# One decoder layer: the dense products handed out in double portions at every second place of three stages

## Time and profile before

| what | value |
|---|---|
| median of three runs | 1400.93 us (1395.85 to 1408.07) |
| the profiled execution | 1402.41 us |
| its span, first to last instruction | 1400.5 us |
| mean granted TensorE clock, as a share of full speed | 0.957 |
| PE matmuls | 1294.8 us busy, 92% of the span |
| DVE, ACT, POOL | 635.9, 350.2 and 578.0 us busy |
| chain that ended last, share of PE | 84% |
| transfers from HBM | 129.31 MB, 92 GB/s on average |

### The profile page before, as it was taken

One profiled execution on the slowest core, in us unless ns is written; L12 is line 12 of the kernel. 1 busy time (PEld: TensorE's weight loads), 2 busy tenths in 40 slices (PEclk: granted clock), 3 DMA queues, 4 the chain that ended last, 5 costly groups with the idle time before them and its releaser, 6 DMA issues.

```text
span 1400.5 us, 23708 instructions
## 1 busy us (share of the span) xinstructions
PE 1294.8 (92%) x10276; PEld 1205.1 (86%) x10276; DVE 635.9 (45%) x1026; ACT 350.2 (25%) x518; POOL 578.0 (41%) x433
## 2 busy tenths in 40 slices
PE   4989999997858899999997999897999999999999
PEld 4989999886758787877787988886999999999999
DVE  6245655525364444455554532314738710177400
ACT  4231222200451233332322121211332211222210
POOL 1443653311163167656512334221536544455542
PEclk9999999997998898999998999988999999999999
DMA  4311121040322143332341325213222323223232
GB/s 181 105 61 61 60 62 56 36 98 31 105 61 93 38 153 127 137 120 76 106 161 50 113 69 196 61 46 122 91 91 91 91 91 91 91 91 93 95 97 95
DMA packets 42909, 129.31 MB, mean 92 GB/s; under 512 B 3958, under 2 KB 15006, under 8 KB 40621
## 3 DMA queue, kind: packets, MB, share of 16 engines
q1 hardware_dynamic: 38197, 102.62, 23.0%
q0 software_dynamic: 4608, 25.17, 5.0%
HBM read 121.64 MB, written 6.36 MB: 91 GB/s over the span
## 4 chain that ended last, share of the span: by engine, by line
PE 84%; DVE 8%; DMA 4%; ACT 2%; issue 1%; SPq 1%; DVEq 0%; ACTq 0%
PE PS L622 19%; PE PS L624 18%; PE PS L623 18%; PE PS L651 9%; PE PS L914 3%; PE PS L937 2%; DMA M<-w_tiles 2%; PE PS L727 2%; PE PS L923 2%; PE PS L1082 1%; PE PS L1070 1%; DMA M<-state_hgrn 1%; PE PS L763 1%; PE PS L765 1%; PE PS L882 1%
## 5 line engine op out<-in xcount | busy, mean ns | idle before, releaser
L2132 POOL TENSOR_TENSOR WL<-M,WH 128x512 fp32r<-128x512 f32 x314 | 426.4, 1382 | 720.2 <-ACT WH L1183 719.8
L622 PE MATMUL PS<-hH,WH 128*128 128x260 f32 x1360 | 406.6, 299 | 23.5 <-DVE M L1470 13.5
L624 PE MATMUL PS<-hH,WL 128*128 128x260 f32 x1360 | 393.0, 289 | 1.5 <-issue 1.5
L623 PE MATMUL PS<-hL,WH 128*128 128x260 f32 x1360 | 393.0, 289 | 0.0
L622 PEld LDWEIGHTS PS<-hH,WH 128*128 128x128 f32 x1360 | 266.5, 196 | 29.8 <-issue 26.2
L624 PEld LDWEIGHTS PS<-hH,WL 128*128 128x128 f32 x1360 | 265.7, 195 | 1.2 <-issue 1.2
L1183 ACT CAST WH<-M 128x1024 fp32r<-128x1024 f32 x159 | 165.9, 1046 | 402.7 <-DMA M<-w_tiles 267.7
L623 PEld LDWEIGHTS PS<-hL,WH 128*128 128x128 f32 x1360 | 266.0, 196 | 0.5
L624 PE MATMUL PS<-uH,WL 128*128 128x260 f32 x512 | 144.7, 283 | 0.0
L622 PE MATMUL PS<-uH,WH 128*128 128x260 f32 x512 | 144.6, 282 | 0.0
L623 PE MATMUL PS<-uL,WH 128*128 128x260 f32 x512 | 144.1, 281 | 0.0
(11 more groups left out here) (368 smaller groups left out, 2088.9 us busy)
## 6 DMA issues: line engine op xcount, KB each, us to landing
M<-w_tiles SPq DMA_DIRECT2D x159, 512.0 KB, 3.6
M<-x_T SPq DMA_DIRECT2D x8, 520.0 KB, 5.5
M<-cache_win_kv SPq DMA_DIRECT2D x2, 2048.0 KB, 11.2
y_T<-M SPq DMA_DIRECT2D x8, 260.0 KB
con<-tables SPq DMA_DIRECT2D x1, 1475.5 KB, 12.1
M<-state_gla SPq DMA_DIRECT2D x2, 512.0 KB, 8.7
M<-state_hgrn SPq DMA_DIRECT2D x2, 512.0 KB, 11.7
gla_sample<-M SPq DMA_DIRECT2D x2, 512.0 KB, 6.8
```

The source lines that it names most:

```text
L622: mm(out, hi[:, cols], x_hi, start=first, stop=False)
L623: mm(out, hi[:, cols], x_lo, start=False, stop=False)
L624: return mm(out, lo[:, cols], x_hi, start=False, stop=last_k)
L2132: last = p.tensor_tensor(WL8[s][:, c], WR[s][:, c], WH8[s][:, c], ALU.subtract)
```

## The change

In the sections lev, att and s6 a tick with an even number within its section hands out twice the quota (16, 8 and 14 triples), and a tick with an odd number none. The other sections keep their quotas. lev and s6 give the same total as before, att gives 272 triples in place of 268; the units and their order are the same. On DVE the calls of ticks 25 and 39 of s6 stand ahead of softmax_of_round in place of behind it.

```diff
-    for _ in range(_n):
-        CUM.append((CUM[-1] if CUM else 0) + _quota)
+    for _i in range(_n):
+        _now = _quota if _name not in ("lev", "att", "s6") else 2 * _quota * (1 - _i % 2)
+        CUM.append((CUM[-1] if CUM else 0) + _now)
...
+            tick("s6", 25)
             softmax_of_round(0, 1)
-            tick("s6", 25)
             tick("s6", 26)
...
+            tick("s6", 39)
             softmax_of_round(1, 0)
-            tick("s6", 39)
             tick("s6", 40)
```

## The result

| what | before | after |
|---|---|---|
| median of the runs | 1401.98 us (4 runs) | 1430.59 us (4 runs) |
| ratio | 1 | 1.0204 [1.0151, 1.0257] |
| the profiled execution, its span | 1400.5 us | 1431.1 us |
| mean granted clock | 0.957 | 0.946 |

The forecast was 1422 with a range of 1392 to 1447: slower, as forecast, and inside the range. But by stage it was right in one place of three. PE by stretch, first before, then after; the stretches are: decay stage (first score group to the first transposes behind it), the unchanged sections up to the attention, attention, samples, the rest. Columns: stretch, its length, PE busy (instructions), PEclk, DMA share, GB/s.

The account below looks back on a forecast made before the run. PE bounds the kernel, so time moves only with its idle, switches and clock. Decay +30.4, attention -18.9 and samples +9.8 give +21.3 on 1402.4, 1423.7; less 1.5 for the median, 1422, range 1392 to 1447.

Parts of the forecast that it names:

- The bank in the decay stage: Second portion of each level: PE waits 1.1 for DVE's eviction behind the products; with POOL's overlap, 23.8 us in all.
- the rate of 0.39: Decay stage: DVE's products run at 0.39 beside POOL's lower parts, making a level's stall 3.05 or 4.7 us.
- The landing of tiles: Decay stage: tiles land 3.6 after release; with a 1.03 cast POOL begins at about 10.3, meeting the products at 10.4.
- The clock in the decay stage: Decay stage: six stalls of 3 us or more each start a clock fall costing 1.6, 9.6 us in all.
- The joins: Joining two portions saves a pair of switches, 0.19 each: decay -3.0, attention -6.3, samples -3.4 us.
- The attention's waits: Attention: PE's waits for blocks of outputs fall from 9.4 to 4.0, about 2 at the first block, 1.9 at the end.
- The clock there: Attention: low clock of 4.3 + 1.6 and 2.9 shrinks to one short fall, -7.2 us.
- The samples: Samples: work ahead of softmax steps delays L980, round 0 and small places; with joins -3.4, +9.8 us, bounds +2 and +18.
- the attention's bound of -13: Attention: the smaller gain, -13 us against the forecast -18.9, if half of the clock stays.
- A: Rival: decay stage nearly free, waits of only 1.1 and no clock fall, +5.8 there, total 1398; chance 0.22.
- B: Rival: faster, DVE's chain in the decay stage is below 5.65 us so the bank costs nothing, total 1379; chance 0.14.
- C: Rival: all eight decay stalls start a long clock fall, 34 us in place of 9.6, total 1447; chance 0.12.

Follow-up runs that it names:

- att_only: Portions of 8 at every second tick in the attention alone, against the kernel before the change: 1400.2 against 1400.35 us, ratio 1.0006.

## Why the prediction was right, and where it was wrong

**The bank in the decay stage: right.** The place (second portion of each level), the releaser and the number of waits came as forecast, and two kernels, one without the third unit in a portion and one with the eviction ahead of the products, have no wait. **Its size was not.** The forecast had 23.8 us, the trace has 13.1. The step that failed is the rate of 0.39: in six levels the products were to last 4.28 to 6.0, they lasted 3.44 to 3.95. In the change the overlap costs the two products 1.1 to 1.6 together, about one instruction of POOL (a tile's lower part is two of them, 2.52 together), though POOL worked beside them to their end. A rate that holds for the whole overlap is not how it goes; the two engines take turns, as the single instructions of the level shown above say:

```profile
172.66 1.41 DVE L1597 TENSOR_TENSOR M<-M 128x1024 f32<-128x1024 f32 x1
172.95 2.27 POOL L2133 TENSOR_TENSOR WL<-M,WH 128x512 fp32r<-128x512 f32 x1
174.00 2.30 DVE L1597 TENSOR_TENSOR M<-M 128x1024 f32<-128x1024 f32 x1
175.18 2.25 POOL L2133 TENSOR_TENSOR WL<-M,WH 128x512 fp32r<-128x512 f32 x1
```

Alone a product takes 1.2 and an instruction of POOL 1.26. Here, from the second row on, each ends 1.08 to 1.15 after the one in the row above it: a product is held until POOL's instruction ends and then has its turn, and POOL's next one is held in the same way. The 4.28 of the earlier trace rows is two products of 2.07 and 2.29, each held once; in the change the second was held for 1.1 and the first for 0.5 at most. The two levels that were to meet no lower part had the short waits (0.8 and 0.7), but level 0 was not one of the dear ones (1.7). The landing of tiles wasn't what set POOL's start: in the level shown above POOL waited 2.96 for ACT's cast, and that cast stood in ACT's list behind the exponential of the distances (1.92 long). Waits, falls and joins give 13.1 + 5.1 - 6.0 = 12.2 of the stage's 13.8; the other 1.6 are not assigned.

**The clock in the decay stage: half right.** Three waits started a fall in place of six; each fall costs about 4.00 x 0.43 = 1.7, the forecast's 1.6. Columns as in the earlier trace rows, two of the three:

```profile
158.50:162.50 4.00, 4.00 (x22) 0.57 0.45 183
179.00:183.00 4.00, 4.00 (x32) 0.57 0.01 4
```

Waits of 2.4, 2.0 and 1.83 were followed by a fall, others of 1.85, 1.81 and 1.74 weren't, and in the kernel with POOL held back none of at most 1.74 was. With the decay stage alone a wait of 2.01 was followed by none and one of 1.79 by one. Which of the middle ones falls, no row here tells.

**The joins: mis-sized in one stage, worth nothing in another.** The step took 0.19 for every join. In the decay stage a join saves 0.36, at the upper bound: 134.05 - 128.03 = 6.0 for 16 (a level in the middle of the stage went from 16.61 to 15.84). In the attention it saves nothing. PE around a join after the change, and around one place of the kernel before without it:

```profile
606.65 0.61 PE L938 MATMUL PS<-M 128*128 128x128 f32 x4
607.19 0.91 PE L915 MATMUL PS<-M 64*128 64x384 f32 x2
```

```profile
588.62 0.28 PE L624 MATMUL PS<-hH,WL 128*128 128x260 f32 x1
588.84 0.91 PE L914 MATMUL PS<-M 64*128 64x384 f32 x2
...
589.95 0.61 PE L937 MATMUL PS<-M 128*128 128x128 f32 x4
590.32 0.37 PE L622 MATMUL PS<-hH,WH 128*128 128x260 f32 x1
590.52 0.28 PE L623 MATMUL PS<-hL,WH 128*128 128x260 f32 x1
```

The four products of L937 start 0.112 apart, the last at 590.29. The first dense one follows after only 0.03, but the second comes 0.20 behind the first: 0.235 for two steps, which is two plain pitches (0.112 + 0.12). So leaving this small group costs nothing. Entering it does: the dense product to L914 takes 0.21, and a join puts the step from the last of L938, at 606.98, to 607.19 in its place, 0.20. So 33 joins give next to nothing (0.01 each) where -6.3 was forecast; the +0.08 each that the expectation of att_only has leaves the second dense step out. Less its waits (9.4, then 9.6), its low clock (5.9, then 7.8) and the 1.4 of the four triples, the stage is 206.5 long before and 206.6 after. The price goes with the step between products over 64 rows (the 64*128 in the rows, L727 and L914) and those over 128, not with the step between dense and small. In the decay stage a whole group is over 64 rows, so a join removes a step in and a step out; in the attention every tick keeps its own. The earlier trace rows showed only the first case, and the 0.19 was carried to a stage whose rows had not been read for it. The Trainium skill has the rule, "TensorEngine Tiling (Array Packing)", section "Key Properties": changing the tiling mode drains TensorE. The trace fits it, if going between 64 and 128 rows is such a change, at about 0.09 to 0.10 above the plain pitch for the step into L727 or L914 and for the one out of L727. What a join saves in the samples isn't settled: the clock differs too much between these traces.

**The attention's waits: right but for one.** The forecast left 4.0 of 9.4, about 2 at the first block and 1.9 at the last; 2.2 and 1.6 are there, with 0.4 at the third. The 1.6 has another cause than forecast: a second branch's lower part (unit 150 now ends at tick 64) stands ahead of the last copies, and the wait at L945 is gone. And it missed the rule that it had used in the decay stage: at tick 34, the second block, a portion ends units 129 and 130 and starts 131, and DVE takes 129 out behind the block of outputs. That wait was 2.5 in the attention alone and 5.4 in the change. DVE and POOL there, and PE's wait:

```profile
609.41 0.24 DVE L1850 RECIPROCAL stat<-stat 128x16 f32<-128x16 f32 x1
609.68 3.13 DVE L1851 TENSOR_TENSOR stat<-stat,wa 128x16 f32<-128x16 f32 x1
...
615.64 0.42 DVE L1476 SCALAR_TENSOR_TENSOR tmp<-tmp,PS 128x260 f32<-128x260 f32 x1
```

```profile
609.31 0.94 POOL L2222 DMA_INDIRECT M<-cache_cmp_kv,idx  x1 [0.30 <-issue]
610.27 2.49 POOL L2133 TENSOR_TENSOR WL<-M,WH 128x512 fp32r<-128x512 f32 x2
```

```profile
616.20 0.56 PE L623 MATMUL PS<-hH,WH 128*128 128x260 f32 x1 [5.39 <-DVE tmp L1476]
```

A product over 128x16 that takes 0.19 elsewhere lasted 3.13 and ended 0.05 after POOL's lower part: it was held, and with it the block, the eviction and PE. **The clock there** was to give 7.2 of 8.8 back. In the stage it cost 7.8 in place of 4.3 + 1.6, since the wait that came in place of the old ones was as long as they were: at half clock after the 5.4 PE was busy 10.30 (0.51), which is 5.0 us, and 5.99 (0.53), 2.8 us, around the first block. Only the 2.9 at the stage's end are gone, with L945's wait.

```profile
557.90:565.10 7.20, 5.99 (x27) 0.53 0.79 286
612.50:626.50 14.00, 10.30 (x36) 0.51 0.28 97
```

The length of this stage is itself uncertain by more than its +2.2: in the nine traces that have it unchanged it is 218.7 to 223.7. What the doubled portions are worth here is what the experiment with the attention alone says, nothing within 0.4%.

**The samples: right.** L980 4.8, as forecast; round 0's chain 3.5 late, forecast 3.9; +8.7 for the stage, forecast +9.8 (the experiment with the samples alone has some 15). In round 1 the 0.9 was too small: the wait grew by 2.0, because a step of 0.35 was held behind POOL's lower part of tile 83. DVE and POOL there:

```profile
939.63 2.50 POOL L2133 TENSOR_TENSOR WL<-M,WH 128x512 fp32r<-128x512 f32 x2 [10.81 <-ACT WH L1184]
939.74 2.46 DVE L1983 TENSOR_TENSOR gaT<-gaT,con 8x64 f32<-8x64 f32 x2 [0.93 <-ACT gaT L1384]
```

L1983 ends when POOL does. With ACT's cast, and so POOL's lower part, moved behind the exponential, the wait is back at 4.7.

**What was not forecast:** 3.5 us in sections whose code and quotas are the same. They come with the clock: 0.90 before, 0.88 after, in the second stretch of the tables above. The same sections are 249.3 long in one experiment's trace and 261.6 in another's:

```profile
235.93:485.27 249.34, 212.47 (x1547) 0.91 0.24 69
```

```profile
242.78:504.38 261.60, 223.87 (x1546) 0.88 0.23 66
```

So the 3.5 is within what one profiled execution differs from another by; that the change causes it isn't shown. So one profile's stage with a mean clock below 1 is a poor measure of a few us. That may also be why the ratio of the samples alone (1.0107) lies above its stage's growth in the change; it isn't shown.

**Two readings of the prediction itself.** The "PE busy 118.9" of the decay stage is not PE's: in the earlier trace rows PE is busy for all 129.0, and 118.93 are its weight loads, so there was no idle time at all to win back. And the attention's bound of -13 doesn't follow from "half of the clock stays", which gives about -15.

**Rivals.** A (decay nearly free) and B (faster) fell on the waits of the decay stage; C (a long fall with every stall) on three short falls. The total lies between the forecast and C, but not by C's mechanism. In the decay stage alone A's +5.8 was nearer to the measured +13.8 than the forecast's +30.4: a wait was 1.6 on average, against A's 1.1 and the forecast's 3.0.

## What to carry to other kernels

When a portion of threaded work grows, count how many units it touches: the unit that starts in the portion in which its bank's last user ended needs that eviction at once, and whatever stands ahead of the eviction in the other engine's list is then on the path. Placing the portions where the eviction comes first turned +12 into -9 us here (decay stage alone, by the medians). Before a price per switch is multiplied, read the pairs of neighbours on both sides of the change, in each stage, and over two starts, not one: the price belongs to a pair of shapes, and work that is moved together gets a new neighbour.

## What the runs showed of the hardware

A DVE product with both operands in SBUF can be held until an instruction of POOL ends, whatever its own size: two over 8x64 took 1.23 and 1.30 in place of 0.35 together, each to the end of one instruction, and two over 128x1024 took 1.41 and 2.30 in place of 1.2 each, in turns with POOL. One over 128x16 (0.19) lasted 3.13 and one over 128x260 (0.43) 3.25: these were held past two instructions of the lower part. The reciprocal of one operand ahead of L1851 took its 0.24. The Trainium skill has it in "SBUF — State Buffer", section "Who interferes with whom": a DVE instruction with two inputs from SBUF contends with one of GpSimd that reads SBUF, and whoever issues later is blocked. The rows of L1983 and L1597 agree with both. In the two long cases the product started 0.59 and 0.42 ahead of the lower part, while POOL was issuing an indirect transfer (DMA_INDIRECT, 0.94); what held it from then on isn't shown. So what POOL's work costs is not a share of DVE's time: a long instruction of POOL can cost each small DVE step of a chain a whole instruction, and only when they meet.
